# Six modulation pieces of layer two computed in another stage, and finer interleaving of the first products

## The chip, the cores and the metric

The kernel runs on one core of a Trainium2 chip. The metric is the device time of one execution in microseconds. Five engines run their own instruction streams: TensorE (PE, with its weight loads as PEld), VectorE (DVE), ScalarE (ACT), GpSimd (POOL) and SyncE (SP), which here only issues DMAs. They are ordered against each other by semaphores alone.

## The reference, cut to what matters

One inference step of a trunk with two layers. Layer one mixes tokens with a gated long convolution (Hyena), layer two with a state-space scan (SSD). Each is followed by an expert-choice mixture of 16 experts. Every sub-layer is modulated by six vectors that come from the conditioning:

```python
def _adaln(cond, ada_w, ada_b):
    m = jax.nn.silu(cond) @ ada_w + ada_b
    return jnp.split(m[:, None, :], 6, axis=-1)
...
    for i in range(DEPTH):
        sh1p, sc1p, g1p, sh2p, sc2p, g2p = _adaln(c_ctx[None, :], ada_w[i], ada_b[i])
        sh1s, sc1s, g1s, sh2s, sc2s, g2s = _adaln(c, ada_w[i], ada_b[i])
        hp = _modulate(_rmsnorm(xp, norm_g[i, 0]), sh1p, sc1p)
        hs = _modulate(_rmsnorm(xs, norm_g[i, 0]), sh1s, sc1s)
...
        xp = xp + g2p * _expert_choice_ffn(_modulate(_rmsnorm(xp, norm_g[i, 1]), sh2p, sc2p), *moe)
```

`ada_w` is 2 x 1024 x 6144 floats. There are 128 context tokens and 1024 latent ones, 1152 together, in nine tiles of 128.

## The kernel before, in words

The program is a row of stages; between two of them all engines meet at a barrier. In order: `phase_front` (conditioning, filter network, norm of layer one), `phase_hyena_in` (first projection), `phase_long_conv`, `phase_hyena_out` (which also scores the experts), `phase_choose` and `phase_experts` for layer one, `phase_norm` of layer two, `phase_ssd_in`, `phase_scan`, `phase_route` and `phase_experts` for layer two, `phase_final`.

**Pieces.** The 12 x 512 columns of `ada_w` of each layer are 24 pieces. A piece is loaded as 2 MB and multiplied by TensorE in 32 products into four blocks of 32 rows (`Modulation.product`, L164). The first four belong to the front. The other twenty stand in the first projection, one behind each of the 24 column tiles q = 0 to 19 (`LAST` = 20), through a ring of four slots (`early_ring`). VectorE adds the bias row (L857); pieces 12 to 15 (shift and scale of layer two's norm) are turned into columns; the others are stored by SyncE as rows in DRAM, `vec_dram` (L719). Pieces 16 and 17 are the gate after layer two's mixer; 18 to 23 are shift, scale and gate of layer two's mixture, read again only in the last stages.

**Projections.** Products run as three passes of a leading and a trailing part (`product3`, L62) over 8 blocks k, in three thirds of 384 tokens: 24 products for a third of a column tile. While the norm's tiles are still being made, thirds stand between the turns of the tiles: a turn is eight transposes on TensorE (L372 in the front, L583 in the norm). Each turn waits until ScalarE and VectorE have emptied the banks of the turn before. `THIRDS_BEHIND` says which third stands behind which tile.

**Norm of layer two.** SyncE loads tiles of x into a ring of four; behind tile `LOADS_BEHIND` it also issues the first SSD weights (`ssd_first`). ScalarE squares, takes the root (L529), empties half of a turn (L538) and makes the leading part (L545); it also rounds the weights (L557, L560) at the tiles given by `DT_SPLIT_AT` and `SPLIT_AT`.

**Choice.** In `phase_choose` VectorE picks the slots (a chain of max, index and replace), TensorE turns four small tables, and VectorE writes them out. SyncE loads the six weight pieces of expert 0 (`keep["ring"]`, `mix_ring` in the profile, L1993), and does not wait for them. `phase_experts` opens with loads of the gates (L2298, L2300), a gather by GpSimd (L2319), a turn of the rows (L2347) and then the gate and up products (L2367).

## Time and profile before

| what | us |
|---|---|
| median of 3 runs | 3720.36 |
| lowest and highest | 3720.31, 3724.67 |
| the profiled execution | 3719.02 |
| its span, first to last instruction | 3717.2 |
| TensorE busy | 3377.8 (91%) |
| VectorE busy | 1863.2 (50%) |
| ScalarE busy | 1282.5 (35%) |

The shares are means over stages with different limits. To judge a stage, read its own stretch: the busy time of each engine there, what TensorE waits for, and which transfer or instruction comes last. The stages that the diff touches lie at about 33 to 88 us (front), 89 to 430 (first projection), 912 to 951 (choice) and 1733 to 1790 (norm of layer two).

### The profile page before, as it was taken

The numbers are of one execution on the slowest core, as the hardware profiler recorded it, in microseconds if no ns is written. First come the engines' busy times: TensorE is split into PE (matmuls) and PEld (weight loads), VectorE is DVE, ScalarE is ACT, GpSimd is POOL, SyncE is SP. The second block draws the span as 40 slices with busy tenths as digits, with TensorE's granted clock in tenths as the row PEclk, the third lists the DMA queues.
The fourth block names the chain that finished last, engine by engine and source line by source line (L and its number), as shares of the span: only waits on it lengthen the run. The fifth ranks groups of instructions, "written<-read, shape, count | busy, mean of one in ns | idle before, by whom it ended". The sixth has DMA issues, their size and how long they took to land. (4 is left out here: it accounts for less than half of the span.)

```text
span 3717.2 us, 58914 instructions
## 1 busy us (share of the span) xinstructions
PE 3377.8 (91%) x24087; PEld 2910.3 (78%) x24087; DVE 1863.2 (50%) x3038; ACT 1282.5 (35%) x2056; POOL 368.8 (10%) x359
## 2 busy tenths in 40 slices
PE   5999898977699999996999999689995699999995
PEld 4999674755699999995899999556663699999995
DVE  5333487766433333333444554699996433333333
ACT  4322323232133233334433223266763133333333
POOL 0000000000111111111010000000000111111111
PEclk8999898988899999997999999899997799999998
DMA  6666313254688888884143443487776488888885
GB/s 237 225 201 202 131 47 126 104 202 173 232 292 291 288 288 287 287 288 137 54 142 107 149 150 102 165 324 252 257 238 265 161 290 287 287 287 288 288 288 188
DMA packets 414216, 799.49 MB, mean 215 GB/s; under 512 B 22039, under 2 KB 108892, under 8 KB 412763
## 3 DMA queue, kind: packets, MB, share of 16 engines
q1 hardware_dynamic: 384940, 700.50, 53.5%
q0 software_dynamic: 28928, 96.96, 8.9%
q8 instruction: 96, 1.57, 0.2%
q14 instruction: 44, 0.36, 0.0%
q10 hardware_dynamic: 208, 0.10, 0.0%
HBM read 688.59 MB, written 108.90 MB: 215 GB/s over the span
## 5 line engine op out<-in xcount | busy, mean ns | idle before, releaser
L2367 PEld LDWEIGHTS moe_banks<-moe_xt,mix_ring 128*128 128x128 f32 x8192 | 1011.4, 191 | 5.5 <-issue 3.2
L2367 PE MATMUL moe_banks<-moe_xt,mix_ring 128*128 128x144 f32 x8192 | 1012.7, 287 | 3.1 <-ACT moe_xt L2402 3.1
L62 PE MATMUL ssd_banks<-h_leading,ssd_w_split 128*128 128x384 f32 x1920 | 415.9, 345 | 1.5 <-DVE ssd_w_split L3033 1.5
L2447 DVE TENSOR_TENSOR moe_hid<-moe_banks,moe_sg 128x128 f32<-128x128 f32 x256 | 74.7, 292 | 580.1 <-ACT moe_sg L2425 580.1
L2389 PE MATMUL moe_banks<-moe_down_parts,moe_hid_parts 128*128 128x512 f32 x1536 | 357.6, 392 | 0.0
L62 PEld LDWEIGHTS ssd_banks<-h_leading,ssd_w_split 128*128 128x128 f32 x1920 | 338.3, 189 | 16.1 <-issue 13.6
L2389 PEld LDWEIGHTS moe_banks<-moe_down_parts,moe_hid_parts 128*128 128x128 f32 x1536 | 285.8, 188 | 71.4 <-issue 13.2
L2437 DVE TENSOR_TENSOR moe_down_parts<-mix_ring,moe_down_parts 128x2048 fp32r<-128x2048 f32 x128 | 292.2, 2283 | 0.0
L3314 PE MATMUL scan_banks<-scan_w,scan_yc 128*128 128x512 f32 x576 | 254.8, 596 | 0.0
L2334 POOL DMA_INDIRECT x_dram<-moe_yc,mix_idx_quarter x128 | 166.5, 1301 | 816.9 <-DVE moe_yc L2458 787.7
L62 PE MATMUL hyin_early_banks<-h_leading,hyin_early_w_split 128*128 128x384 f32 x1152 | 244.2, 339 | 0.9 <-PEq L100 0.9
L2410 ACT ACTIVATE moe_down_parts<-mix_ring 128x2048 fp32r<-128x2048 f32 x128 | 242.6, 1895 | 0.0
L2425 ACT ACT_TABLE_LOAD x32 | 41.1, 1283 | 535.6 <-PE moe_banks L2367 535.6
L62 PE MATMUL ssd_banks<-h_trailing,ssd_w_split 128*128 128x384 f32 x960 | 222.0, 337 | 0.0
L3042 DVE SCALAR_TENSOR_TENSOR ssdin_mid<-ssdin_pad,prm,ssdin_mid 128x1154 f32<-128x1154 f32 x96 | 136.5, 1421 | 156.5 <-ACT ssdin_mid L2907 154.0
L2425 ACT ACTIVATE moe_sg<-moe_banks 128x144 f32<-128x144 f32 x256 | 74.6, 291 | 392.1 <-PE moe_banks L2367 391.8
L62 PEld LDWEIGHTS hyin_early_banks<-h_leading,hyin_early_w_split 128*128 128x128 f32 x1152 | 203.8, 189 | 2.9 <-issue 2.6
L2463 DVE SCALAR_TENSOR_TENSOR moe_yr<-moe_banks,mix_gate_lat,moe_g 128x512 f32<-128x512 f32 x64 | 48.0, 751 | 311.8 <-PE moe_banks L2389 311.8
L3314 PEld LDWEIGHTS scan_banks<-scan_w,scan_yc 128*128 128x128 f32 x576 | 107.3, 191 | 122.3 <-issue 122.3
L62 PEld LDWEIGHTS ssd_banks<-h_trailing,ssd_w_split 128*128 128x128 f32 x960 | 172.1, 188 | 0.0
L62 PE MATMUL hyin_early_banks<-h_trailing,hyin_early_w_split 128*128 128x384 f32 x576 | 137.0, 337 | 0.0
L1812 PE MATMUL hyout_banks<-hyout_w_parts,hyout_g_parts 128*128 128x512 f32 x432 | 104.3, 399 | 19.8 <-DVE hyout_g_parts L1848 19.8
(460 smaller groups left out, 4381.6 us busy)
## 6 DMA issues: line engine op xcount, KB each, us to landing
mix_ring<-in_moe_w_gate SPq DMA_DIRECT2D x64, 2048.0 KB, 8.1
mix_ring<-in_moe_w_up SPq DMA_DIRECT2D x64, 2048.0 KB, 13.0
mix_ring<-in_moe_w_down SPq DMA_DIRECT2D x64, 2048.0 KB, 9.0
early_ring<-in_ada_w SPq DMA_DIRECT2D x84, 512.0 KB, 5.8
scan_cum<-row_dram SPq DMA_DIRECT2D x36, 1024.0 KB, 6.4
ssd_w<-in_ssd_in_w SPq DMA_DIRECT2D x40, 512.0 KB, 4.2
s_dram<-ssdin_work SPq DMA_DIRECT2D x64, 256.0 KB, 3.5
scan_states<-s_dram SPq DMA_DIRECT2D x32, 512.0 KB, 7.7
```

The lines of the kernel that those rows point to most:

```text
L62: ins = pe.matmul(out(piece), w_at(w[a], k), h_k(h[b], k, piece), start=(k == 0 and a == 0 and b == 0), stop=(k == KD - 1 and a == 1))
L1812: ins = pe.matmul(pb[:, 2 * (t % 2) + half, :], g_parts[:, t % 2, a, k, :], w_parts[:, b, k, half * HALF:(half + 1) * HALF], start=(k == 0 ...
L2334: pool.indirect_dma_start(io["x_dram"].rearrange("t (a c) -> (t a) c", a=4), bass.IndirectOffsetOnAxis(ap=keep["idx_quarter"][:, j, e:e + ...
L2367: ins = pe.matmul(pb[:, 2 * (f % 2) + j, 0:SLOTS], ring[:, 2 * half + j, k, col:col + P], xt[:, k, :], start=(k == 0), stop=(k == KD - 1))
L2389: ins = pe.matmul(pb[:, LAT_BANK[half], :], hid_parts[:, a, k, :], wd[:, half, b, k, :], start=(k == 0 and a + b == 0), stop=(k == KD - 1 ...
L2410: act.activation(wd[:, half, 0, ks, :], ring[:, 4 + half, ks, :], ACT.Copy).then_inc(s_wh, 1)
L2425: act.activation(sg[:, f % 2, :], pb[:, 2 * (f % 2), 0:SLOTS], ACT.Silu).then_inc(s_sg, 1)
L2437: dve.tensor_tensor(wd[:, half, 1, ks, :], ring[:, 4 + half, ks, :], wd[:, half, 0, ks, :].bitcast(F32), ALU.subtract).then_inc(s_wl, 1)
L2447: dve.tensor_tensor(hid[:, f % 2, :], up[:, 0:CAP_LAT], sg[:, f % 2, 0:CAP_LAT], ALU.mult).then_inc(s_hid, 1)
L2463: dve.scalar_tensor_tensor(yr[:, cols], pb[:, LAT_BANK[half], :], keep["gate_lat"][:, bass.ds(e, 1)], g2[:, cols], ALU.mult, ALU.mult).the ...
L3042: ins = dve.scalar_tensor_tensor(mid[:, b, :], pad[:, b, tap:tap + GAPPED], prm[:, 0, at:at + 1], mid[:, b, :], ALU.mult, ALU.add)
L3314: ins = pe.matmul(pb[:, out_bank(t) + half, :], yc[:, n % RING, j, :], w[:, k, half * HALF:(half + 1) * HALF], start=(k == 0), stop=(k == ...
```

## The change

It does four things.

- `LATE_PIECES = 6`: the pieces 18 to 23 are no longer made in the first projection (`LAST` is 14), with their loads, products, bias additions and six of the eight stores of layer two's vectors.
- `phase_choose` makes them: SyncE loads them into a ring of five slots (the sixth waits for the first product), TensorE multiplies them ahead of the choice's own transposes, ScalarE clears the rows and loads bias and gains by DMAs of its own, VectorE adds the bias behind its chain, and SyncE stores three vectors for two conditionings, and waits for them at the end.
- The thirds behind tiles 5 to 8 are halved over k, in the front and in the norm of layer two.
- In the norm the SSD weights stand behind the fourth tile of x instead of the second, their rounding stands two tiles later, and ScalarE takes one dummy root ahead of the first tile.

```diff
+LATE_PIECES = 6
...
-        THIRDS_BEHIND = {5: ((0, 0),), 6: ((1, 0),), 8: ((0, 1), (1, 1))}
+        FIRST, SECOND = range(0, KD // 2), range(KD // 2, KD)
+        THIRDS_BEHIND = {5: ((0, 0, FIRST),), 6: ((0, 0, SECOND),), 7: ((1, 0, FIRST),),
+                         8: ((1, 0, SECOND), (0, 1, range(KD)), (1, 1, range(KD)))}
...
-        LOADS_BEHIND, DT_SPLIT_AT, SPLIT_AT = 1, 1, 2
-        THIRDS_BEHIND = {5: ((None, 0),), 6: ((0, 0),), TILES - 1: ((None, 1), (0, 1))}
+        LOADS_BEHIND, DT_SPLIT_AT, SPLIT_AT = RING - 1, 3, 4
+        FIRST, SECOND = range(0, KD // 2), range(KD // 2, KD)
+        THIRDS_BEHIND = {5: ((None, 0, FIRST),), 6: ((None, 0, SECOND),), 7: ((0, 0, FIRST),),
+                         8: ((0, 0, SECOND), (None, 1, range(KD)), (0, 1, range(KD)))}
...
+                act.activation(junk[:, 0:1], keep["eps"][:, 0:1], ACT.Sqrt).then_inc(s_warm, 1)
+                act.wait_ge(s_warm, 1)
...
-        LAST = 2 * 12 - FRONT_PIECES
+        LAST = 2 * 12 - FRONT_PIECES - LATE_PIECES
...
             @block.sync
             def _(sp):
-                for j in range(PIECES):
+                def load_expert(j):
                     sp.dma_start(keep["ring"][:, j, :, :], expert_piece(io, layer, j, 0)).then_inc(keep["s_ring"][j], 16)
+
+                for n in range(LATE_PIECES):
+                    if n == SLOTS:
+                        for j in range(2):
+                            load_expert(j)
+                    at = (FIRST - 12 + n) * HALF
+                    if n >= SLOTS:
+                        sp.wait_ge(s_acc, n - SLOTS + 1)
+                    sp.dma_start(ring[:, n % SLOTS, :, :], ada[:, :, at:at + HALF]).then_inc(s_ada[n], 16)
+                for j in range(2, PIECES):
+                    load_expert(j)
+                sp.wait_ge(s_row, 1)
+                for n, which in enumerate((V_B2, V_A2, V_G2)):
+                    for c in range(2):
+                        sp.dma_start(row_blocks(io["vec_dram"][1, c, which]), rows[c::32, 2 * n:2 * n + 2, :]).then_inc(s_vec, 16)
+                sp.wait_ge(s_vec, 96)
+
+            @block.scalar
+            def _(act):
+                act.activation(rows[:, 0:4, :], keep["tri"][:, 0:4, :], ACT.Copy, scale=0.0).then_inc(s_zero, 1)
+                act.activation(rows[:, 4:8, :], keep["tri"][:, 0:4, :], ACT.Copy, scale=0.0).then_inc(s_zero, 1)
+                act.wait_ge(s_zero, 2)
+                for c in range(2):
+                    act.dma_start(rows[c::32, 0:LATE_PIECES, :], row_blocks(io["ada_b"][1])[:, FIRST - 12:, :]).then_inc(s_bias, 16)
+                    act.dma_start(rows[c::32, GAINS:GAINS + 2, :], row_blocks(io["norm_g"][1, 1])).then_inc(s_bias, 16)
...
+                for n in range(LATE_PIECES):
+                    pe.wait_ge(s_ada[n], 16)
+                    for k in range(KD):
+                        for j in range(4):
+                            ins = pe.matmul(pb[32 * j:32 * j + 32, 1 + n // IN_BANK, n % IN_BANK * P:(n % IN_BANK + 1) * P],
+                                            keep["cond_t"][:, k, :], ring[:, n % SLOTS, k, j * P:(j + 1) * P],
+                                            start=(k == 0), stop=(k == KD - 1))
+                    ins.then_inc(s_acc, 1)
                 choice.turn(pe)
...
                 choice.choose(dve, ch)
+                dve.wait_ge(s_acc, LATE_PIECES)
+                dve.wait_ge(s_bias, 64)
+                for bank, (a, b) in enumerate(((0, IN_BANK), (IN_BANK, LATE_PIECES))):
+                    dve.tensor_tensor(rows[:, a:b, :], pb[:, 1 + bank, 0:(b - a) * P].rearrange("p (n w) -> p n w", w=P),
+                                      rows[:, a:b, :], ALU.add).then_inc(s_add, 1)
+                dve.wait_ge(s_add, 2)
+                dve.scalar_tensor_tensor(rows[:, 2:4, :], rows[:, 2:4, :], 1.0, rows[:, GAINS:GAINS + 2, :],
+                                         ALU.add, ALU.mult).then_inc(s_row, 1)
                 choice.tables(dve)
```

SyncE's instructions of the choice and of the start of the expert stage, before (a name is the tile written, then the tensor read, then the shape):

```order
L1993 DMA mix_ring<-in_moe_w_gate 128x8x512
L1993 DMA mix_ring<-in_moe_w_up 128x8x512
L1993 DMA mix_ring<-in_moe_w_gate 128x8x512
L1993 DMA mix_ring<-in_moe_w_up 128x8x512
L1993 DMA mix_ring<-in_moe_w_down 128x8x512 x2
L1988 UNCONDITIONAL_BRANCH
L2296 UNCONDITIONAL_BRANCH
L2298 DMA moe_g<-vec_dram 128x1024
```

The same place on SyncE, after:

```order
L2018 DMA choose_late_pieces<-in_ada_w 128x8x512 x5
L2009 DMA mix_ring<-in_moe_w_gate 128x8x512
L2009 DMA mix_ring<-in_moe_w_up 128x8x512
L2018 DMA choose_late_pieces<-in_ada_w 128x8x512
L2009 DMA mix_ring<-in_moe_w_gate 128x8x512
L2009 DMA mix_ring<-in_moe_w_up 128x8x512
L2009 DMA mix_ring<-in_moe_w_down 128x8x512 x2
L2024 DMA vec_dram<-choose_late_rows 4x2x128 x6
L2004 UNCONDITIONAL_BRANCH
L2353 UNCONDITIONAL_BRANCH
L2355 DMA moe_g<-vec_dram 128x1024
```

Six loads of pieces stand among the six of expert 0, and six stores behind all of them, ahead of the end of the stage (the branches).

SyncE's instructions of the norm of layer two, before:

```order
L514 DMA norm_x<-x_dram 128x1024 x2
L2552 DMA ssd_wdt<-in_ssd_in_w 128x8x64
L2553 DMA ssd_head_columns<-in_ssd_dt_bias 64x1
L2554 DMA ssd_head_columns<-in_ssd_A_log 64x1
L2545 DMA ssd_w<-in_ssd_in_w 128x8x128 x3
L514 DMA norm_x<-x_dram 128x1024 x7
```

And after:

```order
L520 DMA norm_x<-x_dram 128x1024 x4
L2609 DMA ssd_wdt<-in_ssd_in_w 128x8x64
L2610 DMA ssd_head_columns<-in_ssd_dt_bias 64x1
L2611 DMA ssd_head_columns<-in_ssd_A_log 64x1
L2602 DMA ssd_w<-in_ssd_in_w 128x8x128 x3
L520 DMA norm_x<-x_dram 128x1024 x5
```

The third and fourth tile of x have moved ahead of the weights.

## Rows read from the trace of the kernel before

**Rows 1.** Busy time by window: first projection, then one expert's period.

```profile
core 0: us, PE busy (x) PEld busy (x) DVE busy (x) ACT busy (x) POOL busy (x), PEclk, DMA share, GB/s
270.00:372.00 102.00, 102.00 (x961) 98.90 (x959) 32.78 (x32) 27.70 (x39) 4.04 (x5) 1.00 0.63 209
...
1011.25:1058.70 47.45, 47.45 (x385) 43.78 (x384) 16.11 (x31) 14.55 (x24) 8.69 (x7) 1.00 0.83 289
```

**Rows 2.** Timeline of TensorE in the first projection: start, duration, engine, line, operation.

```profile
355.50 1.95 PE L164 MATMUL hyin_early_banks<-early_ring,cond_t 128*32 128x128 f32 x64
357.38 0.33 PE L769 MATMUL hyin_early_banks<-tri,hyena_work 128*128 128x128 f32 x1
```

**Rows 3.** Choice: SyncE's issues, their time to landing, and the rate.

```profile
911.92 0.38 SPq L1993 DMA_DIRECT2D mix_ring<-in_moe_w_gate  x1
...
922.30 10.63 SPq L1993 DMA_DIRECT2D mix_ring<-in_moe_w_down  x2
...
DMA to landing us min/median/max: 8.6/18.4/20.1
...
mix_ring<-in_moe_w_down SPq DMA_DIRECT2D x2, 2048.0 KB, 19.9
...
920.00:945.00 25.00, 0.00 (x0) 0.00 (x0) 24.22 (x57) 0.00 (x0) 0.00 (x0) 0.50 1.05 387
```

**Rows 4.** Timelines of four engines from the choice into the expert stage.

```profile
950.64 0.40 DVE L1976 TENSOR_SCALAR mix_idx_quarter<-choose_banks 16x16 uint32<-16x16 f32 x4
...
951.68 0.34 SPq L2298 DMA_DIRECT2D moe_g<-vec_dram  x1
...
952.42 1.03 POOL L2319 DMA_INDIRECT moe_xe<-h_dram,mix_idx_lat  x1 [50.77 <-POOLq L100]
...
957.61 1.97 PE L2347 MATMUL moe_banks<-tri,moe_xe 128*128 128x128 f32 x8 [7.34 <-DMA moe_xc<-h_dram,mix_idx_ctx]
...
962.07 33.16 PE L2367 MATMUL moe_banks<-moe_xt,mix_ring 128*128 128x144 f32 x256 [1.53 <-ACT moe_xt L2402]
```

**Rows 5.** DMA issues, KB and us to landing: norm of layer two, then projection's end.

```profile
ssd_wdt<-in_ssd_in_w SPq DMA_DIRECT2D x1, 256.0 KB, 5.0
ssd_head_columns<-in_ssd_dt_bias SPq DMA_DIRECT2D x1, 0.2 KB, 4.7
...
early_negt<-in_negt SPq DMA_DIRECT2D x1, 9.0 KB, 1.8
```

**Rows 6.** Norm of layer two: timelines of ScalarE and of TensorE.

```profile
1738.13 1.28 ACT L529 ACT_TABLE_LOAD   x1
...
1746.12 1.06 ACT L527 ACTIVATE norm_junk<-norm_x 128x1024 f32<-128x1024 f32 x1 [5.03 <-DMA norm_x<-x_dram]
...
1740.77 1.97 PE L583 MATMUL ssd_banks<-tri,norm_xn 128*128 128x128 f32 x8 [16.56 <-DVE norm_xn L599]
1749.09 1.94 PE L583 MATMUL ssd_banks<-tri,norm_xn 128*128 128x128 f32 x8 [6.35 <-ACT norm_h L538]
...
1761.02 1.94 PE L583 MATMUL ssd_banks<-tri,norm_xn 128*128 128x128 f32 x8 [1.77 <-ACT norm_h L538]
1764.73 1.94 PE L583 MATMUL ssd_banks<-tri,norm_xn 128*128 128x128 f32 x8 [1.76 <-ACT norm_h L538]
...
1772.63 1.03 PE L583 MATMUL ssd_banks<-tri,norm_xn 128*128 128x128 f32 x8
...
1780.35 1.06 PE L583 MATMUL ssd_banks<-tri,norm_xn 128*128 128x128 f32 x8 [1.64 <-ACT norm_h L538]
```

**Rows 7.** Front: timeline of TensorE, and ScalarE's emptying of tile 7.

```profile
70.67 1.03 PE L372 MATMUL hyin_early_banks<-tri,hyena_work 128*128 128x128 f32 x8
...
75.71 1.03 PE L372 MATMUL hyin_early_banks<-tri,hyena_work 128*128 128x128 f32 x8
78.74 1.06 PE L372 MATMUL hyin_early_banks<-tri,hyena_work 128*128 128x128 f32 x8 [1.99 <-ACT front_h L301]
...
76.79 1.86 ACT L301 ACTIVATE front_h<-hyin_early_banks,shift,gain 128x128 f32<-128x128 f32 x5 [2.24 <-PE hyin_early_banks L372]
```

More of the change, by code:

```diff
@@ L336, in _, with project @@
             def _(pe):
-                def project(q, piece):
+                def project(q, piece, ks):
                     pe.wait_ge(s_wl, q + 1)
@@ L342, in project @@
                              (split[:, q, 0, :, :], split[:, q, 1, :, :]), lambda w_, k: w_[:, k, :],
-                             keep["h_parts"], third, pieces=(piece,))
+                             keep["h_parts"], third, ks, (piece,))
                 pe.wait_ge(keep["s_const"], 16)
@@ L375, in _ @@
                     if t in THIRDS_BEHIND:
-                        for q, piece in THIRDS_BEHIND[t]:
-                            project(q, piece)
+                        for q, piece, ks in THIRDS_BEHIND[t]:
+                            project(q, piece, ks)
             @block.vector
@@ L563, in _, with project @@
             def _(pe):
-                def project(q, piece):
+                def project(q, piece, ks):
                     if q is None:
@@ L573, in project @@
                     parts = [dt_split[:, part, :, :] if q is None else split[:, 0, part, :, :] for part in range(2)]
-                    product3(pe, out, parts, lambda w_, k: w_[:, k, :], keep["h_parts"], third, pieces=(piece,))
+                    product3(pe, out, parts, lambda w_, k: w_[:, k, :], keep["h_parts"], third, ks, (piece,))
                 for t in range(TILES):
@@ L586, in _ @@
                     if t in THIRDS_BEHIND:
-                        for q, piece in THIRDS_BEHIND[t]:
-                            project(q, piece)
+                        for q, piece, ks in THIRDS_BEHIND[t]:
+                            project(q, piece, ks)
             @block.vector
@@ L707, in _ @@
             def _(sp):
-                for layer in range(2):
-                    for c in range(2):
-                        sp.dma_start(rows[c::32, 2 * layer:2 * layer + 2, :], row_blocks(io["norm_g"][layer, 1])).then_inc(s_gin, 16)
+                for c in range(2):
+                    sp.dma_start(rows[c::32, 0:2, :], row_blocks(io["norm_g"][0, 1])).then_inc(s_gin, 16)
                 def vectors(layer):
                     at = 12 * layer
-                    sp.wait_ge(s_row, 12 * (layer + 1) - FRONT_PIECES)
-                    sp.wait_ge(s_ar, 2 * layer + 2)
-                    for which, n in ((V_G1, 4), (V_B2, 6), (V_A2, 8), (V_G2, 10)):
+                    sp.wait_ge(s_row, LAST if layer else 12 - FRONT_PIECES)
+                    sp.wait_ge(s_ar, 2)
+                    for which, n in ((V_G1, 4), (V_B2, 6), (V_A2, 8), (V_G2, 10))[:1 if layer else 4]:
                         for c in range(2):
@@ L732, in _ @@
                         vectors(1)
[L733 removed]
+                mod.finished(sp, 23 - LATE_PIECES)
                 conv_first(sp, io, keep)
[L735 removed]
+                sp.wait_ge(s_vec, 16 * 10)
                 sp.wait_ge(s_cv, HY_TILES)
@@ L857, in piece, with a_rows @@
                     dve.tensor_tensor(rows[:, n, :], piece_out(q), rows[:, n, :], ALU.add).then_inc(s_row, 1)
-                def a_rows(layer):
-                    if layer == 0:
-                        dve.wait_ge(s_gin, 64)
-                    dve.wait_ge(s_row, 12 * layer + 10 - FRONT_PIECES)
-                    at = slice(12 * layer + 8, 12 * layer + 10)
-                    dve.scalar_tensor_tensor(rows[:, at, :], rows[:, at, :], 1.0, rows[:, 2 * layer:2 * layer + 2, :],
+                def a_rows():
+                    dve.wait_ge(s_gin, 32)
+                    dve.wait_ge(s_row, 10 - FRONT_PIECES)
+                    dve.scalar_tensor_tensor(rows[:, 8:10, :], rows[:, 8:10, :], 1.0, rows[:, 0:2, :],
                                              ALU.add, ALU.mult).then_inc(s_ar, 2)
@@ L878, in _ @@
                         piece(q)
-                    for layer in range(2):
-                        if q == 12 * layer + 10 - FRONT_PIECES:
-                            a_rows(layer)
+                    if q == 10 - FRONT_PIECES:
+                        a_rows()
                     dve.wait_ge(s_mid, q + 1)
@@ L1986, in phase_choose @@
         s_dve = m.sem("dve")
+        FIRST = 2 * 12 - LATE_PIECES
+        GAINS, IN_BANK, SLOTS = LATE_PIECES, 4, 5
+        ada = io["ada_w"][1].rearrange("(k p) n -> p k n", p=P)
+        ring = m.sb("late_pieces", [P, SLOTS, KD, HALF])
+        rows = m.sb("late_rows", [P, LATE_PIECES + 2, P])
+        s_ada = [m.sem(f"piece_in{n}") for n in range(LATE_PIECES)]
+        s_zero = m.sem("rows_zero")
+        s_bias = m.sem("bias_in")
+        s_acc = m.sem("pieces_summed")
+        s_add = m.sem("bias_added")
+        s_row = m.sem("rows_ready")
+        s_vec = m.sem("vectors_stored")
         with nc.Block() as block:
```

4 lines of the change are left out of this document (2 added, 2 removed).

## The prediction

> **What bounds the kernel now.** I read the windows of busy time first, to see in which stretch which engine is the limit, then the timeline of TensorE, VectorE, ScalarE and SyncE at the three places that the diff touches, and last the DMA issues with their time to landing.
>
> In the first projection TensorE is the limit: it is busy for all 102.0 of the 102.0 us between 270 and 372, while the DMA engines are at 0.63 of theirs and VectorE and ScalarE at about a third [rows 1]. So what TensorE no longer does there comes off the span, and the loads of the pieces there are free.
>
> In the choice of the first expert stage it is the other way round. TensorE does nothing from 912 on until the slots are chosen. VectorE's chain ends at 951.04 (950.64 + 0.40), SyncE issues the first load of the expert stage at 951.68, GpSimd gathers at 952.42, TensorE turns rows at 957.61 and starts the gate and up products at 962.07 [rows 4]. Beside that chain SyncE's queue brings the six weight pieces of the first expert, at 387 GB/s [rows 3]. The reader should work out how full that queue is: the first piece is issued at 911.92 and lands 8.6 us later, at 920.5. The two down pieces are the fifth and sixth; their issues take 10.63 us together, so the sixth starts at 927.6, and with 19.9 us to landing it lands at about 947.5. That is (947.5 - 920.5) / 5 = 5.4 us for each piece of 2 MB, one behind the other. The stage ends 3.5 us after the last of them, and nothing in it waits for them. So this stage has an idle TensorE to offer, but hardly any idle time of the queue.
>
> In the norm of layer two ScalarE waits 5.03 us for the third tile of x, and TensorE's second turn (1749.09) comes 8.3 us after its first [rows 6]; from there a tile takes 3.7 us (1761.02 to 1764.73). The third of the products that stands whole between two turns then pushes the turns back.
>
> **The change part by part.**
>
> *Six pieces leave the projection.* A piece takes TensorE 357.38 - 355.50 = 1.88 us, with no gap on either side [rows 2]. Six take 11.3. The stretch stays bound by TensorE without them, since q 20 to 23 already run without a piece in the same way. Six of the eight stores of layer two's vectors go too (on SyncE, hidden). **-11.3**, between -11.0 and -11.5.
>
> *Halved thirds in the front.* Now the turns of tiles 6, 7 and 8 stand at 70.67, 75.71 and 78.74 [rows 7]. A third of 24 products takes 75.71 - 70.67 - 0.8 of the turn = 4.2, its half 2.1. The turn of tile 6 now stands behind a first third; with halves it stands 2.1 earlier, at 68.6. ScalarE, after its work on tile 8, can empty it from about 70.1 on, in 1.86, and so tile 7 is turned at 72.0, behind the second half. Tile 8 is turned when tile 7 is emptied, at 75.1. That is 3.6 us earlier than 78.74, but 2.1 us more of products now stand behind it: **-1.5**. Bounds: 0 (other work fills the gap) and -2.0, the gap ahead of 78.74.
>
> *Norm of layer two.* The four first tiles of x now stand ahead of the SSD weights. Before, everything up to the third tile was in by 1746.1; the fifth tile, the first that stands behind the weights, has two tiles more ahead of it, at about 1.35 us each by 512 KB at 387 GB/s, so it is in at about 1748.8. Until then ScalarE handles tiles 0 to 3 without a wait: turns at 1739.5, 1743.1, 1746.7, and then 1751.8, 1756.0 and 1760.7, the last two with 0.5 and 1.0 us of weight splits between them. The sixth turn stands at 1760.7 against 1764.73. The product behind it is cut in half, so the seventh stands at 1766.1 against 1772.63, the eighth at 1769.3, the ninth at 1772.2 against 1780.35. Behind the ninth stand 2.1 us more of products than before: 8.15 - 2.1 = **-6**. The preloaded root table (1.28 us [rows 6]) moves the first turns only: the fifth tile arrives later than ScalarE is ready either way. Bounds: -3.5, if only the earlier tiles count and the halves bring nothing, and -7.
>
> *The choice.* TensorE multiplies six pieces in its idle time: at the lower of its two clocks 64 of these products take at most twice the 1.88 us, less than the 5.4 between landings. VectorE adds four short operations behind its chain, ScalarE two and four DMAs of its own. What counts is SyncE's queue. It now carries twelve transfers of 2 MB: five pieces, two expert weights, the sixth piece, four expert weights. At 5.4 us they land at 920.5 + 5.4 (n - 1): the sixth piece, eighth in the row, at 958.3, the last expert weight at 979.9. Behind that weight SyncE waits for the rows (ready at about 963), issues six stores of 4 KB into the same queue and, at the end of the stage, waits until they have landed. No engine passes the end of the stage before that.
>
> When do they land? An issue into a full queue ends only when an earlier transfer has gone: the sixth ended at 932.9, some 1.6 us after the third had landed, so the twelfth ends near 965. The stores would then be free to go, but stand behind 15 us of loads. [rows 5] say what that means: the DMA of 0.2 KB (dt bias) issued right behind 256 KB of weights and two tiles took 4.7 us to land, as long as the 5.0 of the 256 KB ahead of it; one of 9 KB into a quiet queue took 1.8. A small transfer lands right behind what stands ahead of it. So the stores land at about 980.5, the stage ends, and with the same 0.64 as before (951.04 to 951.68) SyncE starts the expert stage at 981.2 instead of 951.68. Everything of the expert stage shifts with it: **+29.5**; with up to 1.5 more for the stores' own way I take **+30**. Bounds: +19, if the stores pass the loads (965.3, plus 6 x 0.5 of issue, plus 1.8, plus 0.64 = 970.7, against 951.68), and +33, if they take a whole 4.7 behind the last weight.
>
> Once the stage begins, all weights of expert 0 are in, and an expert's period (47.45 us, DMA share 0.83 [rows 1]) is TensorE's as before; nothing is given back there, because TensorE was never waiting for weights.
>
> The Trainium skill, page "DMA: Bandwidth & Descriptors", section "Queues, rings and completion order", says that each DMA engine takes descriptors in the order of a queue's ring, but that completion is not first in, first out over a whole issuing engine, as a small DMA may sit on few rings. By the first half the sum is the one above; by the second the stores may overtake whatever ring lags, and that is the first rival below. The rows of 0.2 KB agree with the first half.
>
> **The sum.** -11.3 - 1.5 - 6 + 30 = +11.2. The profiled execution took 3719.02 us (span 3717.2), 1.3 below the median of 3720.36; on the median that gives **3731.6 us**.
>
> **Rivals.**
> *The stores are not held back.* Place: SyncE's queue between 965 and 981. If small stores pass the loads, the shift is 19 and the total 19 - 18.8 = +0.2: 3720.6, no change. For it: they write, while all ahead of them reads, and they touch few partitions. Against it: [rows 5]. The point: a landing at 977 (a shift of 26.2 and a total of +7.4) divides slower from no change; before 970 the total turns negative.
> *The gains at the norm and the front do not arrive.* If the halves bring nothing (front 0, norm -3.5), the sum is +15.2: 3735.6. For it: each term rests on several engines keeping step over five tiles. Against it: each start was worked out from measured durations.
> *The stores cost nothing, only the sixth piece does.* If the store wait were met during VectorE's chain, only the wait for the sixth piece would remain: 958.3, up to 4.3 for its products at the lower clock, 1 for VectorE, 0.64: 964.2, a shift of 12.5 and a total of -6.3: 3714.1; with products at the higher clock 2 less, 3712. Against it: the wait is in the code, behind all issues. It holds only if neither the queue's order nor the order of issue counts.
>
> **How the numbers follow.** Forecast 0.68, gains that do not arrive 0.14, stores not held back 0.12, the last case 0.06. The bounds of the single terms around the forecast (30 within +28.5 and +33, norm within -5 and -7) make 3729 to 3736. The range takes in the second rival and part of the way to the first: 3725 to 3738. A measurement of this kernel can tell some 0.2%, 7.4 us, from no change. Slower by over that: the forecast and the second rival, 0.80; within it: the first rival, the edge of the forecast and most of the last case, 0.16; faster: the rest of the last case, 0.04.
>
> **What the changed profile would show.** In the choice: twelve landings 5.4 us apart, TensorE multiplying behind each of six of them, VectorE ready near 964, then all engines idle until near 981, and the first expert's gate products at about 992 before the earlier stages' gains are taken off. In the projection: 11.3 us less from 89 to 430, and TensorE still busy throughout. In the norm: no wait of 5 us on ScalarE, the ninth turn some 8 us earlier counted from the stage's start. The prediction is wrong if the stores land well before the last expert weight, if the loads run at another pace than 5.4 us a piece, or if the expert stage's first periods are longer or shorter than 47.5.

## The result, and the profile after

Seven runs of each kernel side by side gave 3733.05 us for the changed one (3732.06 to 3735.02) and 3722.7 us for the one before (3719.19 to 3724.67). The ratio is 1.003, with a 95% interval from 1.002 to 1.0039: slower by 7 to 15 us. The prediction was 3731.6, with 3725 to 3738 as its range; its change was +11.2, that of the medians is +10.35. The profiled execution of the changed kernel took 3734.91 us, its span 3733.0.

To see where the time went I took the start of the same instruction in both traces at the end of every stage. All numbers are "after minus before", in us:

| up to | shift | this stage |
|---|---|---|
| first piece behind the front (TensorE) | -1.35 | -1.35 |
| last turn of the first projection (TensorE) | -13.92 | -12.57 |
| first load of the choice (SyncE) | -13.59 | +0.33 |
| first load of the expert stage (SyncE) | +17.05 | +30.64 |
| first gate product (TensorE) | +17.81 | +0.76 |
| first load of the norm of layer two (SyncE) | +18.42 | +0.61 |
| end of the norm: first weight split of the SSD stage (ScalarE) | +12.54 | -5.88 |
| end of the scan: eighth of its nine stores of x (SyncE) | +12.98 | +0.44 |

**Projection.** The first answer below is the changed kernel's busy time by window, where the first row answers to the first of [rows 1]. The second and third are the turns between the projection's pieces (count, duration, start of the first and of the last), of the changed kernel and of an experiment that keeps all pieces (halved thirds, no piece moved, below).

```profile
256.00:358.00 102.00, 102.00 (x700) 101.00 (x699) 33.71 (x31) 29.41 (x43) 4.58 (x6) 1.00 0.36 112
```

```profile
L776 PE MATMUL hyin_early_banks<-tri,hyena_work x36: 270/272/301, 293.8 to 413.1; 128*128 128x128 f32 x36
```

```profile
L776 PE MATMUL hyin_early_banks<-tri,hyena_work x36: 270/273/330, 294.6 to 424.4; 128*128 128x128 f32 x36
```

TensorE is still busy for all 102.0 of 102.0 us; the DMA share fell from 0.63 to 0.36, because the loads of the pieces are gone. With pieces the 36 turns take 129.8 us from first to last, without them 119.3. Five of the six pieces lie between these turns (the first lies ahead of the first turn), so a piece is worth 10.6 / 5 = 2.1.

**The choice.** SyncE's timeline of the changed kernel, where [rows 3] and [rows 4] stood before, then its issues with KB and time to landing, and the rate by window (the last number is GB/s):

```profile
898.33 16.04 SPq L2018 DMA_DIRECT2D choose_late_pieces<-in_ada_w  x5
914.41 5.49 SPq L2009 DMA_DIRECT2D mix_ring<-in_moe_w_gate  x1
919.94 5.29 SPq L2009 DMA_DIRECT2D mix_ring<-in_moe_w_up  x1
925.28 4.45 SPq L2018 DMA_DIRECT2D choose_late_pieces<-in_ada_w  x1
929.78 6.78 SPq L2009 DMA_DIRECT2D mix_ring<-in_moe_w_gate  x1
936.60 5.29 SPq L2009 DMA_DIRECT2D mix_ring<-in_moe_w_up  x1
941.93 10.60 SPq L2009 DMA_DIRECT2D mix_ring<-in_moe_w_down  x2
952.57 7.83 SPq L2024 DMA_DIRECT2D vec_dram<-choose_late_rows  x6
968.73 0.34 SPq L2355 DMA_DIRECT2D moe_g<-vec_dram  x1
```

```profile
mix_ring<-in_moe_w_down SPq DMA_DIRECT2D x2, 2048.0 KB, 19.8
```

```profile
900.00:940.00 40.00, 17.03 (x320) 13.98 (x320) 34.63 (x90) 0.00 (x0) 0.00 (x0) 0.59 1.04 385
940.00:966.00 26.00, 4.17 (x68) 3.39 (x68) 2.11 (x13) 0.00 (x0) 0.00 (x0) 0.50 1.02 376
966.00:970.00 4.00, 0.00 (x0) 0.00 (x0) 0.00 (x0) 0.00 (x0) 0.53 (x1) 0.50 0.10 24
```

The last weight is issued near 947.2. Its own landing is not in the trace; with the 19.8 of the one before it, it lands at 967.0. The rate stays at 376 to 385 GB/s until 966 and is 24 after it. The stores are issued from 952.57 on, and the stage ends at 968.1 (968.73 less the 0.64 of [rows 4]), 1.1 behind the last weight. All six are issued by 960.4, so the last 8 us are the wait for their landing, not for a place in the queue. The engines that compute were ready long before. These are VectorE's last row of the stage, and TensorE's last piece and first turn of the expert stage:

```profile
950.84 0.40 DVE L1980 TENSOR_SCALAR mix_idx_quarter<-choose_banks 16x16 uint32<-16x16 f32 x4
```

```profile
945.38 3.64 PE L2042 MATMUL choose_banks<-choose_late_pieces,cond_t 128*32 128x128 f32 x64 [12.60 <-DMA choose_late_pieces<-in_ada_w]
...
975.42 1.97 PE L2404 MATMUL moe_banks<-tri,moe_xe 128*128 128x128 f32 x8 [25.86 <-DMA moe_xc<-h_dram,mix_idx_ctx]
```

VectorE is done at 951.24. From there to 968.1 nothing computes: 17 us of standing still, in which the only thing left is a queue that empties.

**The norm of layer two.** ScalarE's preloaded table and its one wait for x, then TensorE's turns, where [rows 6] stood before:

```profile
1751.72 1.28 ACT L553 ACT_TABLE_LOAD   x1 [22.63 <-PEq L100]
...
1767.80 1.06 ACT L533 ACTIVATE norm_junk<-norm_x 128x1024 f32<-128x1024 f32 x1 [1.82 <-DMA norm_x<-x_dram]
```

```profile
1757.94 1.97 PE L591 MATMUL ssd_banks<-tri,norm_xn 128*128 128x128 f32 x8 [15.46 <-DVE norm_xn L607]
1761.55 1.94 PE L591 MATMUL ssd_banks<-tri,norm_xn 128*128 128x128 f32 x8 [1.64 <-ACT norm_h L544]
...
1779.64 1.94 PE L591 MATMUL ssd_banks<-tri,norm_xn 128*128 128x128 f32 x8 [2.71 <-ACT norm_h L544]
1784.12 1.03 PE L591 MATMUL ssd_banks<-tri,norm_xn 128*128 128x128 f32 x8
...
1790.59 1.06 PE L591 MATMUL ssd_banks<-tri,norm_xn 128*128 128x128 f32 x8 [0.36 <-DVE norm_h L615]
```

The wait of 5.03 us for the third tile is gone; one of 1.82 for the fifth took its place. Less the shift of 18.42, the ninth turn stands at 1772.17 against 1780.35 before.

**The front.** TensorE's turns of tiles 6 to 8, where [rows 7] stood before:

```profile
69.14 1.12 PE L375 MATMUL hyin_early_banks<-tri,hyena_work 128*128 128x128 f32 x8
72.25 1.07 PE L375 MATMUL hyin_early_banks<-tri,hyena_work 128*128 128x128 f32 x8
75.46 1.06 PE L375 MATMUL hyin_early_banks<-tri,hyena_work 128*128 128x128 f32 x8
```

These are two executions. Over all twelve kernels here the first piece behind the front stands at 93.0 to 94.2 in the three with whole thirds in the front, and at 90.8 to 92.3 in the nine with halves.

Behind the scan the code is the same in both kernels, and from the scan's eighth store of x to the output of the prompt it took 898.6 us before and 901.4 after in the profiled executions; 2.4 of the 2.8 more lie in layer two's route. These two rows, of the kernel before and of the changed one, are the same part of layer two's route, TensorE's granted clock third from the end:

```profile
2845.00:2858.00 13.00, 8.25 (x110) 1.00 1.04 412
```

```profile
2858.30:2871.30 13.00, 9.96 (x98) 0.75 1.04 412
```

This is not the change's doing: in the ten experiments below, with and without it, the same stretch took 898.4 to 902.2. So I compare the two traces only up to the scan's end, +12.98, which lies inside the measured interval; the spans (15.8 apart) hold 2.8 us of chance.

### The profile page after: what moved, and what is told of

Its sections match the earlier page's. It is cut to its first block and busy times, and to the rows that moved or that the text cites. A ratio compares the mean times of both kernels' runs of the same rounds, so it can differ in the third digit from the quotient of the medians.

```text
span 3733.0 us, 58903 instructions
## 1 busy us (share of the span) xinstructions
PE 3394.6 (91%) x24087; PEld 2924.2 (78%) x24087; DVE 1862.0 (50%) x3034; ACT 1283.6 (34%) x2059; POOL 368.7 (10%) x359
## 5 line engine op out<-in xcount | busy, mean ns | idle before, releaser
L62 PEld LDWEIGHTS ssd_banks<-h_leading,ssd_w_split 128*128 128x128 f32 x1920 | 339.2, 189 | 16.1 <-issue 13.6
```

What stands on the lines that cost most here:

```text
L62: ins = pe.matmul(out(piece), w_at(w[a], k), h_k(h[b], k, piece), start=(k == 0 and a == 0 and b == 0), stop=(k == KD - 1 and a == 1))
```

## The experiments

Ten kernels ran, each timed against the kernel before. The first four ask whether the terms add up, and what holds the end of the choice.

**Pieces moved, thirds whole.** The changed kernel with the thirds, the order of loads and the root table as before.

```diff
...
-        LOADS_BEHIND, DT_SPLIT_AT, SPLIT_AT = RING - 1, 3, 4
...
+        LOADS_BEHIND, DT_SPLIT_AT, SPLIT_AT = 1, 1, 2
...
-                act.activation(junk[:, 0:1], keep["eps"][:, 0:1], ACT.Sqrt).then_inc(s_warm, 1)
```

> The changed kernel with the thirds whole again in front and norm, the weights behind the second tile, no preloaded root: only the move of the six pieces is left. Theory: the parts add up. The projection gains 12.5 us (426.99 to 413.08 at the last turn, less 1.4 of the front), the choice costs 31.4 (from the stage's start to the first gate product), so +18.9 against the kernel before, some 3741.6, a ratio of 1.0051. Rival: the move itself is neutral and the rise of the changed kernel comes from the finer thirds or from a place not looked at: a ratio below 1.002.

Measured: 3739.05 us (3737.81 to 3744.2), ratio 1.0052 [1.0038, 1.0065]. Moving the pieces alone costs 14 to 24 us.

**Thirds halved, no piece moved.** The kernel before with the rest of the change.

```diff
-        THIRDS_BEHIND = {5: ((0, 0),), 6: ((1, 0),), 8: ((0, 1), (1, 1))}
+        FIRST, SECOND = range(0, KD // 2), range(KD // 2, KD)
+        THIRDS_BEHIND = {5: ((0, 0, FIRST),), 6: ((0, 0, SECOND),), 7: ((1, 0, FIRST),),
+                         8: ((1, 0, SECOND), (0, 1, range(KD)), (1, 1, range(KD)))}
...
-        LOADS_BEHIND, DT_SPLIT_AT, SPLIT_AT = 1, 1, 2
+        LOADS_BEHIND, DT_SPLIT_AT, SPLIT_AT = RING - 1, 3, 4
...
+                act.activation(junk[:, 0:1], keep["eps"][:, 0:1], ACT.Sqrt).then_inc(s_warm, 1)
```

> The kernel before with only the halved thirds, the order of loads and the preloaded root of the change; all twenty pieces stay in the projection. Theory: front -1.4, norm -5.9, in sum -7.3, some 3715.4, a ratio of 0.9980. Rival: these gains exist only while the rest of the program is shifted, or are given back behind the norm: a ratio between 0.9995 and 1.0005.

Measured: 3715.15 us (3711.75 to 3717.94), ratio 0.9984 [0.9975, 0.9993]: faster than the kernel before by 3 to 9 us. The parts add: 1.0052 x 0.9984 = 1.0036, and the whole change measured 1.003 [1.002, 1.0039]. This part is a gain, the other a loss.

**Sixth piece ahead of the expert weights.** Two places in SyncE's order.

```diff
-                    if n == SLOTS:
-                        for j in range(2):
-                            load_expert(j)
...
-                for j in range(2, PIECES):
+                for j in range(PIECES):
```

> The changed kernel with the sixth piece ahead of all expert weights, so that it lands at about 934 instead of 945 and the rows are ready some 9 us sooner. The number of transfers is the same. Theory: the stage ends behind the whole queue, so nothing moves, 0 +- 0.5 us against the changed kernel, stage end near 968.7. Rival (the late sixth piece and the products and additions behind it set the end): -9 to -10.8 us, 3723.

Measured: 3734.17 us (3732.84 to 3735.32), ratio 1.0035 [1.0022, 1.0049], which can't be told from the changed kernel's. VectorE's and SyncE's timelines of it:

```profile
937.43 0.40 DVE L1980 TENSOR_SCALAR mix_idx_quarter<-choose_banks 16x16 uint32<-16x16 f32 x4
```

```profile
897.22 21.52 SPq L2015 DMA_DIRECT2D choose_late_pieces<-in_ada_w  x6
...
951.67 7.78 SPq L2021 DMA_DIRECT2D vec_dram<-choose_late_rows  x6
967.77 0.34 SPq L2352 DMA_DIRECT2D moe_g<-vec_dram  x1
```

Rows and tables are ready at 937.8, 40.6 us after the stage's start instead of 52.9, and the stage still takes 70.55 us where it took 70.40. So no engine's work and no wait for the sixth piece sets its end.

**The stores on ScalarE's queue.** The six stores and the wait for them move from SyncE's program to ScalarE's.

```diff
             def _(sp):
...
-                sp.wait_ge(s_row, 1)
...
             def _(act):
...
+                act.wait_ge(s_row, 1)
...
+                        act.dma_start(row_blocks(io["vec_dram"][1, c, which]), rows[c::32, 2 * n:2 * n + 2, :]).then_inc(s_vec, 16)
+                act.wait_ge(s_vec, 96)
```

> The changed kernel with the six stores of the late vectors, and the wait for them, on ScalarE's queue instead of SyncE's. All loads stay as they are. Theory (order in SyncE's queue): the stores land about 3 us after their issue at 951 to 954, SyncE has issued its last load at 952.6, the stage ends near 957.5 and the expert stage starts at 958.2 instead of 968.7: -10.5 us against the changed kernel, some 3722.5, no change against the kernel before. Rival (the 16 DMA engines are simply full until 967, whatever queue a store is in): the stage still ends near 968, 0 to -2 us.

Measured: 3726.27 us (3722.96 to 3733.12), ratio 1.0014 [1.0005, 1.0023]. Below are ScalarE's, SyncE's, GpSimd's and TensorE's rows of it.

```profile
950.65 3.35 ACTq L2033 DMA_DIRECT2D vec_dram<-choose_late_rows  x6
```

```profile
942.13 10.59 SPq L2009 DMA_DIRECT2D mix_ring<-in_moe_w_down  x2
959.11 0.34 SPq L2355 DMA_DIRECT2D moe_g<-vec_dram  x1
```

```profile
959.85 1.03 POOL L2376 DMA_INDIRECT moe_xe<-h_dram,mix_idx_lat  x1 [72.03 <-POOLq L100]
```

```profile
968.37 1.97 PE L2404 MATMUL moe_banks<-tri,moe_xe 128*128 128x128 f32 x8 [18.96 <-DMA moe_xc<-h_dram,mix_idx_ctx]
```

On the other queue the stores don't wait for the loads: the stage ends 9.4 us earlier counted from its start, with the last weights still on their way. But only 7 arrive at the end. The gather of rows (959.85 to TensorE's turn at 968.37) took 8.5 us among the loads, where the changed kernel's took 5.95 (969.47 to 975.42) with none of the 2 MB loads beside it.

The next three take the wait away by moving work, and ask how much of the price of the choice can be had back.

**Stores in the expert stage.** The rows stay on the core, the six stores go behind the start of the expert stage, and the gates' loads move to ScalarE's queue. The edit also puts the sixth piece ahead of the expert weights, which the expectation does not say; by the experiment with the sixth piece first, this alone brings nothing. The two kernels after it do the same.

```diff
-        rows = m.sb("late_rows", [P, LATE_PIECES + 2, P])
+        rows = keep["late_rows"]
...
-                    if n == SLOTS:
-                        for j in range(2):
-                            load_expert(j)
...
-                for j in range(2, PIECES):
+                for j in range(PIECES):
...
+                if layer == 0:
+                    for n, which in enumerate((V_B2, V_A2, V_G2)):
+                        for c in range(2):
+                            sp.dma_start(row_blocks(io["vec_dram"][1, c, which]), keep["late_rows"][c::32, 2 * n:2 * n + 2, :]
+                                         ).then_inc(s_vec, 16)
```

> The changed kernel with only the six stores of rows and the wait for them moved from the choice to the expert stage of layer one; all twelve loads of 2 MB (six pieces, six expert weights) stay in the choice. Theory (the end of the choice is set by where the stores stand in SyncE's queue, and behind that by the time at which SyncE can issue its last load): the twelfth issue ends near 952.6 of the changed kernel's trace, so the expert stage starts near 953.3 instead of 968.7, 15.4 earlier; the gather loses some 2.5 to the loads that are still on their way: 13 gained, 3720. Rival (bytes set it): as with the stores on ScalarE's queue, 3726.

Measured: 3721.47 us (3719.22 to 3724.92), ratio 1.0002 [0.9993, 1.0011]. The whole loss is gone. Its SyncE:

```profile
941.81 10.63 SPq L2009 DMA_DIRECT2D mix_ring<-in_moe_w_down  x2
953.33 9.80 SPq L2352 DMA_DIRECT2D vec_dram<-mix_late_rows  x6
```

The stage now takes 55.4 us (897.90 to 953.33), 15.0 less than in the changed kernel, and ends with the issue of the last weight, which is held up until 952.4, though that weight is used only behind the first expert's gate and up products, and these take over 30 us. So its place in SyncE's program holds up a stage that doesn't wait for its landing.

**Down weights in the expert stage too.** The diff is against the kernel with the stores moved.

```diff
-                for j in range(PIECES):
+                for j in range(4):
                     load_expert(j)
...
+                    for j in range(4, PIECES):
+                        sp.dma_start(ring[:, j, :, :], expert_piece(io, layer, j, 0)).then_inc(s_ring[j], 16)
```

> The changed kernel with two things taken out of the choice and put into the expert stage of layer one: the six stores of rows with the wait for them (the rows stay in the cores' own memory for the stage), and the two down weights of the first expert. SyncE issues six pieces and four expert weights in the choice and no more. Theory (the changed kernel's choice ends when its last expert weight has landed, because the stores stand behind it in SyncE's queue): the last of ten issues now ends near 941 of the changed kernel's trace, VectorE's tables are ready near 941 too, so the expert stage starts near 942 instead of 968.7, 27 earlier; the gather then meets a queue that is still full and takes some 3 us more than in the changed kernel, as it did with the stores on ScalarE's queue: 24 gained, 3733.1 - 24 = 3709. Rival 1 (the sixth piece and VectorE's work behind it set the end by themselves): rows are ready near 951, 16 gained, 3717. Rival 2 (what is loaded is what costs: 12 transfers of 2 MB are on the queue and the expert stage waits for them, whatever stands in which stage): no more than the 7 us that the ScalarE queue gave, 3726.

Measured: 3710.2 us (3709.11 to 3711.05), ratio 0.9969 [0.9957, 0.9981]. Expected was 3709; both rivals (3717, 3726) fall. It beats the kernel before. Whether the move of the pieces pays is less sure: the median is 5 below that of the halved thirds alone (3715.15), and from the choice's start to the first gate product this kernel takes 8.1 more than the kernel before, for 12.6 saved in the projection. But the two intervals overlap. SyncE's and TensorE's rows:

```profile
899.11 21.59 SPq L2015 DMA_DIRECT2D choose_late_pieces<-in_ada_w  x6
...
943.52 13.49 SPq L2351 DMA_DIRECT2D mix_ring<-in_moe_w_down  x2
```

```profile
957.34 34.58 PE L2422 MATMUL moe_banks<-moe_xt,mix_ring 128*128 128x144 f32 x256 [1.53 <-ACT moe_xt L2457]
```

From the first load to the first gate product it takes 58.2 us, the changed kernel 81.55 and the kernel before 50.15 [rows 3, 4].

**The gather first.** Against the kernel before this one two more weights move, and SyncE waits for the gather before it issues them.

```diff
-                for j in range(4):
+                for j in range(2):
...
+                    sp.wait_ge(s_xe, 32)
+                    for j in range(2, PIECES):
```

> The kernel with the down weights and the stores moved into the expert stage, and two more of the first expert's weights moved there: the choice issues six pieces and two expert weights, and in the expert stage SyncE issues the four others and the stores only when the first gather of rows has landed. Theory (what is left of the change's price is VectorE's own time for the tables and the gather's share of a queue that is still full, 9.4 us from the stage's start to TensorE's turn instead of 5.9): VectorE is ready 41.4 after the choice's start, so the stage starts at 42.1 instead of 44.4; the eighth load lands at 46.4, so the gather shares the queue for 4 us only and takes near its 5.9; the first gate product starts at 52 to 53 after the choice's start instead of 58.2. The second half's weights land 57 and 62 after it, needed at 69. 5 to 6 gained on that kernel: 3704 to 3705. Rival (the gather's time doesn't hang on the loads but on the indirect transfer's own way, and the loads that are issued late make TensorE wait in the first expert): stage start 2 earlier and the rest as it was or worse, 3708 to 3712.

Measured: 3707.99 us (3706.82 to 3709.46), ratio 0.9957 [0.9943, 0.997]. This is the fastest kernel here by its median, but the interval overlaps that of the one before it. The forecast of 3704 to 3705 was missed. The median lies at the lower edge of the rival's 3708 to 3712, but neither of its reasons came out: the gather did get shorter, and TensorE did not wait for the late weights. The kernel before this one was timed against runs of 3721.23, this one against 3723.16, so the trace compares the two better: 55.5 us from the choice's start to the first gate product instead of 58.2, where 52 to 53 was forecast.

```profile
941.03 1.03 POOL L2375 DMA_INDIRECT moe_xe<-h_dram,mix_idx_lat  x1 [53.70 <-POOLq L100]
```

```profile
948.62 1.97 PE L2403 MATMUL moe_banks<-tri,moe_xe 128*128 128x128 f32 x8 [10.72 <-DMA moe_xc<-h_dram,mix_idx_ctx]
...
953.08 34.20 PE L2423 MATMUL moe_banks<-moe_xt,mix_ring 128*128 128x144 f32 x256 [1.53 <-ACT moe_xt L2458]
```

```profile
940.00:945.00 5.00, 0.00 (x0) 0.00 (x0) 0.00 (x0) 0.00 (x0) 1.92 (x2) 0.63 1.05 374
945.00:950.00 5.00, 1.38 (x7) 1.39 (x8) 0.27 (x1) 0.00 (x0) 0.00 (x0) 0.50 0.37 108
```

Counted from the choice's start the gather is issued 1.7 us earlier than in the kernel with the down weights moved (43.4 against 45.15). But from its issue to TensorE's turn it took 7.6 us instead of the 8.6 there, though the 2 MB loads ran beside it only up to about 945.5. I had counted on 5.9. Why it stayed longer is open, and part of it may be chance: in the kernel with the order of loads alone (below), whose choice is that of the kernel before, the same gather took 6.9 us with no such load beside it.

```profile
953.32 1.03 POOL L2320 DMA_INDIRECT moe_xe<-h_dram,mix_idx_lat  x1 [50.77 <-POOLq L100]
```

```profile
960.19 1.97 PE L2348 MATMUL moe_banks<-tri,moe_xe 128*128 128x128 f32 x8 [9.02 <-DMA moe_xc<-h_dram,mix_idx_ctx]
```

TensorE's first expert took no longer (34.20 against 34.58), so the late weights made nobody wait.

The last three split the norm.

**Order of loads alone**, on the kernel before:

```diff
-        LOADS_BEHIND, DT_SPLIT_AT, SPLIT_AT = 1, 1, 2
+        LOADS_BEHIND, DT_SPLIT_AT, SPLIT_AT = RING - 1, 3, 4
```

> The kernel before with one part of the change alone: in the norm stage of layer one the loads of x tiles stand ahead of more of the split work (loads behind the third instead of the first, splits at tiles 3 and 4), thirds whole, the table of square roots not loaded ahead, no piece moved. The order and the halves together gave 6.3 us in the comparison of halved thirds and load order against the kernel before, 4.5 to 5 of it in the norm stage by the trace and 1.4 in front. Theory of the prediction (the x tile that arrives late is the wait, and the load order takes it away): 3 to 4.5 gained, ratio 0.9988 to 0.9992. Rival (it is the halves that let TensorE turn a tile before a whole third is through): 0 to 1 gained, ratio 0.9998 to 1.0.

Measured: 3717.08 us (3715.69 to 3721.29), ratio 0.9988 [0.9979, 0.9998], as the prediction's theory said. The norm got 4.4 us shorter (57.23 to 52.87). (The stage is layer two's norm; the expectation calls it layer one's.)

**Halves alone**, on the kernel before: the first diff of the halved thirds above in the front, and in the norm

```diff
-        THIRDS_BEHIND = {5: ((None, 0),), 6: ((0, 0),), TILES - 1: ((None, 1), (0, 1))}
+        THIRDS_BEHIND = {5: ((None, 0, FIRST),), 6: ((None, 0, SECOND),), 7: ((0, 0, FIRST),),
+                         8: ((0, 0, SECOND), (None, 1, range(KD)), (0, 1, range(KD)))}
```

> The kernel before with the halved thirds alone, in the front and in the norm of layer two: loads in their old order, table of square roots not loaded ahead, no piece moved. The load order alone has already shortened the norm stage by 4.4 us (57.2 to 52.9 from the first load of x to the first weight split of the SSD stage), the whole edit by 5.9, of which the root table is 1.4. Theory now: the halves bring nothing in the norm beyond 0.5 and 1.4 in the front: ratio 0.9995 to 0.9997, norm stage 56.7 to 57.3. Prediction's theory (the halves let the last three turns come earlier, about 2 of the 6 us): norm stage near 55, ratio 0.9991.

Measured: 3717.55 us (3716.25 to 3722.04), ratio 0.9987 [0.9978, 0.9996]; the norm took 55.8 us. My later theory (no gain in the norm) falls: the gain is 1.4, less than the 2 that the prediction's step gives.

**No root table ahead**, on the changed kernel:

```diff
-                act.activation(junk[:, 0:1], keep["eps"][:, 0:1], ACT.Sqrt).then_inc(s_warm, 1)
-                act.wait_ge(s_warm, 1)
```

> The changed kernel without the one small square root that ScalarE does at the start of the norm stage, so that the table of square roots is loaded when the first tile needs it. Prediction: it brings nothing to the end, 3733.1, the same as the changed kernel. Rival (the table's load of 1.3 us stands in the chain of the first tile): 1.3 more, 3734.4.

Measured: 3733.12 us (3729.69 to 3735.33), ratio 1.003 [1.002, 1.0041]: the same as the changed kernel. The table below gives the norm's length from SyncE's first load of x to ScalarE's first split of the SSD stage, the start of TensorE's sixth, seventh and ninth turn in it, and the time at which TensorE's granted clock goes from 0.50 (1.2 GHz) to 1.00 (2.4 GHz).

| kernel | norm | turn 6 | turn 7 | turn 9 | clock rises |
|---|---|---|---|---|---|
| before | 57.2 | 31.4 | 39.3 | 47.1 | 37.5 |
| halves alone | 55.8 | 31.7 | 37.3 | 43.5 | 37.3 |
| order alone | 52.9 | 28.1 | 35.0 | 42.7 | 31.9 |
| both, no root ahead | 52.7 | 28.2 | 33.7 | 40.2 | 34.2 |
| changed kernel | 51.4 | 27.9 | 32.4 | 38.9 | 31.1 |

The order brings the sixth turn 3.3 us forward, the halves the ninth by 2.5 to 3.6, of which 2.1 are given back by the product that now stands behind it.

The last column shows what the prediction had no term for. Where ScalarE waits for the third tile of x, TensorE's second turn stands 15.8 to 16.5 us into the norm, and the clock rises at 37.3 to 37.5 (three kernels). With the new order of loads the second turn stands at 9.6 to 10.9, and the clock rises at 30.6 to 34.2 (nine kernels). So part of what the order brings behind the sixth turn comes with a faster TensorE. These are the 10 us that begin 30 us into the norm, of the kernel before and of the order alone, with the granted clock third from the end:

```profile
1763.29:1773.29 10.00, 8.56 (x39) 0.62 0.01 2
```

```profile
1767.10:1777.10 10.00, 10.00 (x57) 0.91 0.00 0
```

With the root ahead the sixth turn stands only 0.2 earlier, as the prediction said, and yet the seventh stands 1.3 earlier. That goes with the clock too, here in the same window of the kernel without the root ahead, then of the changed one:

```profile
1780.54:1790.54 10.00, 10.00 (x53) 0.79 0.00 0
```

```profile
1781.71:1791.71 10.00, 9.64 (x62) 0.95 0.00 0
```

Whether the root is the reason isn't shown. Seven executions with order, halves and root have the rise at 30.6 to 32.1, but the order alone, which has no root ahead either, has it at 31.9; only the one execution with order and halves but no root has 34.2. What the earlier rise brings is given back in the SSD stage, where the same two kernels, in the same order, show the opposite:

```profile
1822.00:1832.00 10.00, 3.76 (x29) 0.85 0.08 22
1832.00:1842.00 10.00, 10.00 (x48) 0.80 0.68 204
```

```profile
1822.00:1832.00 10.00, 4.40 (x30) 0.76 0.07 20
1832.00:1842.00 10.00, 10.00 (x44) 0.73 0.70 206
```

From the norm's start to the scan's eighth store of x both take the same, 1059.03 and 1059.11 us; the kernel before took 1064.55.

## Why the prediction was right

**Pieces out of the projection: right, undersized.** -12.6 instead of -11.3. The stretch stayed bound by TensorE, as said. The term took 1.88 us for a piece, the distance between two starts in [rows 2]; by the turns with and without pieces it is 2.1. The bounds (-11.0 to -11.5) were too narrow: the row gives the 64 products of a piece, and what their place between products of another kind costs stands outside it. I did not take those 0.2 us apart.

**Front: right.** The turns were forecast for 68.6, 72.0 and 75.1 and stand at 69.14, 72.25 and 75.46; the term was -1.5 and is -1.35.

**Norm: right in size, partly by luck.** -5.88 against -6; the ninth turn, forecast for 1772.2, stands at 1772.17 after the shift, and the eight ahead of it within 0.7 of the forecast. But the step gave 3.5 to the order of loads, the other 2.5 to the halves and nothing to the root. The order alone brought 4.4, the halves alone 1.4, both without the root 4.5 (with a clock that rose 2.3 later than with the order alone), and all three 5.9. The step had no term for TensorE's clock, which rose 6.4 earlier in the changed kernel than before; without the root ahead the ninth turn stands 1.2 later than forecast. For the program's end the step was right about the root: it changes nothing there.

**Choice: right, and the reason is shown.** SyncE's expert stage was forecast 29.5 later and is 30.64 later, both counted without the gains ahead of it; with the gather's 0.76 that makes 31.4, against +30 with a bound of +33. Loads landed one behind the other until 967.0, where 979.9 - 13.6 = 966.3 was expected; the stores, issued from 952.57, were through 1.1 behind the last, as the small load of [rows 5] had landed right behind what stood ahead of it. That the stores' place in SyncE's queue does it is shown by three edits that leave the twelve loads as they are: having the rows ready 12.3 earlier brought nothing, another queue for the stores brought 9.4 in the stage, and another stage for them 15.0. *"The stores are not held back"* was therefore wrong for SyncE's queue and true for ScalarE's. *"The stores cost nothing, only the sixth piece does"* fell with the sixth piece put first. The gains at norm and front did arrive.

Two smaller readings came out too: VectorE was to be ready near 964, less the shift of 13.6 at 950.4, and was at 951.24; a piece's products were to take up to twice 1.88 us in the choice, and took 3.64 where TensorE had stood idle for 12.60.

The Trainium skill, page "DMA: Bandwidth & Descriptors", section "Queues, rings and completion order", was cited for both sides: order within a ring, and small transfers that may finish out of it. Here the order decided. The same section says that each DMA engine takes turns between queues, a packet from each, and the section "Issuing engines are not separate DMA queues" says that issuing from several engines saves only the issuing time. The trace agrees as far as bandwidth goes (376 to 385 GB/s with the stores on SyncE's queue, 388 from 950 to 958 with them on ScalarE's). It differs from the second section for a small transfer: on ScalarE's queue the six stores were through 9 us earlier, with the same loads outstanding. Taking turns between queues would give that; no run here shows the turns themselves.

So the errors of the terms are -1.27 (pieces), +1.4 (choice) and +0.27 (front and norm), together +0.4; another 1.38 are small shifts between the stages (0.33, 0.61 and 0.44 in the table), for which the sum had no term. Together that is +12.98 against +11.2. Two of the errors helped each other out. The medians give +10.35; how much of the 12.98 is chance of two single executions isn't known.

## What to carry to other kernels

Before work is put where an engine is idle, draw the line of the queue that has to feed it: a stage in which TensorE sleeps may still have no free microsecond on the queue, and then the moved work costs what its bytes cost (here 12 MB, 30 us, for 12.6 saved). Small transfers whose landing is waited for, and loads that are needed late, don't belong on that queue ahead of the stage's end: moving those, with the sixth piece put first, turned the same change from 1.003 into 0.9969. And split a change into its parts: this one held a gain of 0.2% and a loss of 0.5%.

## What the runs showed of the hardware

- A gather by an indirect DMA took 5.2 to 6.9 us from its issue to TensorE's turn with no 2 MB load beside it (eight kernels), 8.5 to 8.6 with such loads beside it throughout (three kernels), and 7.6 with loads beside it for some 4.5 us (one kernel).
- An issue by SyncE into the full queue took 5.3 us, the time in which one 2 MB load lands, so the end of a stage can be set by the issue of a transfer that nobody there needs (the kernel with the stores moved: 952.4).
- The order of loads ahead of a row of short turns moved the rise of TensorE's clock: 37.3 to 37.5 us into the norm with the old order (three kernels), 30.6 to 34.2 with the new one (nine kernels). A gain that consists of clock need not last: of two kernels one had the rise 3.1 us earlier and a norm 1.4 us shorter, and both took the same to the scan's eighth store (1059.03 and 1059.11).
- The same code behind the scan took 898.4 to 902.2 us in twelve executions of twelve kernels. In the two compared above the granted clock was 1.00 and 0.75 in the same 13 us of layer two's route; that this makes the difference isn't shown.
